# RWKV products stacked into wider matmuls with v centred beforehand, last units by row blocks, own banks for group 0, later root sum for mem

## What is computed

```python
def step(state, inp):                      # RWKV-7, per head, state 64x64
    r_t, w_t, k_t, v_t, a_t, b_t = inp
    sa = einsum('bhij,bhj->bhi', state, a_t)
    state = state * w_t + sa[..., None] * b_t + v_t[..., None] * k_t
    return state, einsum('bhij,bhj->bhi', state, r_t)
...
mean = y.mean(-1); var = ((y - mean) ** 2).mean(-1)
y = (y - mean) * rsqrt(var + B_GN_EPS) * ln_w + ln_b
return (y + sum(r * k * r_k) * v) * g
...
h = h + square(relu(xn @ mlp_w1)) @ mlp_w2
return rms_norm(h, norm_final)
```

## Time and profile before

| | |
|---|---|
| median of 3 runs | 2764.14 us (2763.07 to 2765.19) |
| profiled execution, its own time | 2762.59 us |
| span of that profile | 2760.9 us |
| TensorE busy | 2712.9 us (98%), granted clock 0.996 of 2.4 GHz |
| VectorE, ScalarE, GpSimd busy | 1236.4 (45%), 809.3 (29%), 132.9 us (5%) |

### The profile page before, as it was taken

How to read it: one execution, slowest core, us unless ns; L and a number is a source line. 1 busy time by engine, 2 the same in 40 slices (tenths; PEclk the granted TensorE clock), 3 DMA queues, 4 the chain that set the end, 5 groups by cost and what they waited for, 6 DMA issues and landing times.

```text
span 2760.9 us, 44373 instructions
## 1 busy us (share of the span) xinstructions
PE 2712.9 (98%) x18368; PEld 2158.3 (78%) x18368; DVE 1236.4 (45%) x1895; ACT 809.3 (29%) x1333; POOL 132.9 (5%) x237
## 2 busy tenths in 40 slices
PE   9999999999998999998999999999999999999997
PEld 7877777777777766786888888888888888888885
DVE  6266666666435545344433333333333333333333
ACT  5222222222124444243431221312213222122222
POOL 4000111001121100000000000000000000000000
PEclk9999999999999999999999999999999999999998
DMA  4311111111135422221233223322323323323322
GB/s 162 119 60 49 48 48 52 45 50 50 59 108 197 170 79 62 84 88 51 86 98 99 95 97 99 97 93 99 98 92 99 99 92 98 99 92 98 99 94 112
DMA packets 72396, 249.23 MB, mean 90 GB/s; under 512 B 8960, under 2 KB 9088, under 8 KB 71104
## 3 DMA queue, kind: packets, MB, share of 16 engines
q1 hardware_dynamic: 65232, 222.62, 25.3%
q0 software_dynamic: 7024, 24.56, 2.6%
HBM read 236.93 MB, written 10.22 MB: 90 GB/s over the span
## 4 chain that ended last, share of the span: by engine, by line
PE 94%; DVE 3%; issue 1%; DMA 1%; ACT 1%; DVEq 0%; SPq 0%; POOL 0%; ACTq 0%
PE ps L1141 28%; PE ps L1143 26%; PE ps L1142 26%; PE ps L1159 9%; PE ps L1375 1%; PE ps L1354 1%; PE ps L1363 1%; DMA h<-in_mem_turned 1%; PE ps L1153 1%; DVE w_lo L713 0%; PE ps L1214 0%; PE ps L1205 0%; PE ps L1194 0%; PE ps L1211 0%; PE ps L1220 0%
## 5 line engine op out<-in xcount | busy, mean ns | idle before, releaser
L713 DVE TENSOR_TENSOR w_lo<-w_raw,w_hi 128x1024 fp32r<-128x1024 f32 (+2 forms) x440 | 506.0, 1150 | 1143.4 <-ACT w_hi L432 1143.4
L432 ACT ACTIVATE w_hi<-w_raw 128x1024 fp32r<-128x1024 f32 (+2 forms) x440 | 439.0, 998 | 1539.3 <-PE ps L1143 1531.4
L1141 PE MATMUL ps<-act_hi,w_hi 128*128 128x512 f32 x1792 | 730.1, 407 | 1.1 <-DVE w_lo L713 1.1
L1143 PE MATMUL ps<-act_hi,w_lo 128*128 128x512 f32 x1792 | 700.1, 391 | 0.0
L1142 PE MATMUL ps<-act_lo,w_hi 128*128 128x512 f32 x1792 | 699.2, 390 | 0.0
L1141 PE MATMUL ps<-w_hi,mid_hi 128*128 128x512 f32 x1088 | 424.4, 390 | 1.4 <-DVE mid_lo L1087 1.4
L1143 PE MATMUL ps<-w_hi,mid_lo 128*128 128x512 f32 x1088 | 423.3, 389 | 0.0
L1142 PE MATMUL ps<-w_lo,mid_hi 128*128 128x512 f32 x1088 | 423.3, 389 | 0.0
L1141 PEld LDWEIGHTS ps<-act_hi,w_hi 128*128 128x128 f32 x1792 | 336.2, 188 | 93.7 <-issue 12.0
L1143 PEld LDWEIGHTS ps<-act_hi,w_lo 128*128 128x128 f32 x1792 | 336.5, 188 | 72.1
L1142 PEld LDWEIGHTS ps<-act_lo,w_hi 128*128 128x128 f32 x1792 | 336.8, 188 | 68.9 <-issue 6.0
(11 more groups left out here) (276 smaller groups left out, 2443.3 us busy)
## 6 DMA issues: line engine op xcount, KB each, us to landing
w_raw<-in_w_rest SPq DMA_DIRECT2D x320, 512.0 KB, 3.5
w_raw<-in_w_pairs SPq DMA_DIRECT2D x112, 384.0 KB, 3.0
x_t<-in_x_turned SPq DMA_DIRECT2D x8, 512.0 KB, 8.0
qk<-scr_qkv POOLq DMA_DIRECT2D x16, 256.0 KB, 3.6
h<-in_x POOLq DMA_DIRECT2D x4, 1024.0 KB, 11.1
out<-h SPq DMA_DIRECT2D x4, 1024.0 KB, 4.3
scr_qkv<-pad POOLq DMA_DIRECT2D x15, 256.0 KB, 3.8
w_raw<-in_w_lora SPq DMA_DIRECT2D x8, 288.0 KB, 7.1
```

The costliest lines, as they stand in the source:

```text
L432: return nc.scalar.activation(dst, src, ACT.Copy, scale=scale)
L713: V.tensor_tensor(dst, w_raw[:, slot, 0:dst.shape[-1]], high.bitcast(F32), ALU.subtract).then_inc(s["w_split"], 1)
L1141: mm(dst, a_hi, b_hi, start=start, stop=False)
L1143: return mm(dst, a_lo, b_hi, start=False, stop=stop)
```

## The change

It has six parts.

1. *Stacked products.* k and b lie side by side in `keys_b`. One product with 128 stationary columns (b and k) gives both Gram blocks of a head at once: with a (`gram_a`), with r (`gram_r`), and with the identity (`tok`, both turned to tokens). Each head has a bank of its own. The masks are applied to two banks at once. `keys_b` is written by halves (64 partitions each), so k x g_inv and b x g_inv become two VectorE instructions each.
2. *Chain.* u and v lie one above the other in `uv`. y takes one matmul per head over 128 rows, and so does the state. Bank 7 (`B_CHAIN`) holds all; y is copied out by VectorE after each chunk (L995 of the changed kernel). The v part of the next chunk's z moves from third 0 to the end of `chain_sy`, behind a wait of TensorE on its own y.
3. *Centred v.* v is turned to tokens with a centring matrix (`cen2`, identity less 1/64), which takes the place of the mean matmul, the copy of y and the subtraction for v; u comes out centred with it.
4. *Group 0* writes banks 4 to 6; its row sums move from position 18 to 21, its evacuation to unit 0 of group 1.
5. *mem*: sum over partitions, root and reciprocal move from positions 21 to 23 of group 14 to unit 2 of stage XK.
6. *End*: the gain is loaded early and multiplied into the first three quarters of h in the last chunk; the last two units are worked off by row blocks of 128 tokens, and each row tile is finished and stored by itself, ScalarE scaling 1536 columns, VectorE 512.

```diff
+            def stacked(b, rhs):
+                for c in range(NC):
+                    for hd, hf in enumerate(HALF):
+                        lhsT = keys_b[hf, c, :, :].rearrange("p i t -> p (i t)")
+                        last = mm(ps[:, b + hd, part(c)], lhsT, rhs(hf, c), start=True, stop=True)
+                return last
...
-                    mm(bank(3), mean2[:, :], yb[:, :], start=True, stop=True).then_inc(s["mean_mm"], 1)
...
-                    to_tokens(3, kk_dec).then_inc(s["ktok_mm"], 1)
-                if p == 10 and elem:
-                    pe.wait_ge(s["ab_ready"], q + 1)
-                    pe.wait_ge(s["ss_max"], q + 1)
-                    grams(4, kk_dec, aT[par]).then_inc(s["mak_mm"], 1)
-                if p == 11 and elem:
-                    pe.wait_ge(s["bon_ev"], q + 1)
-                    grams(5, kk_dec, rT[par]).then_inc(s["mrk_mm"], 1)
...
+                if p == 11 and elem:
                     pe.wait_ge(s["kt_ready"], q + 1)
+                    pe.wait_ge(s["ab_ready"], q + 1)
+                    pe.wait_ge(s["bt_ready"], q + 1)
+                    pe.wait_ge(s["ss_max"], q + 1)
+                    pe.wait_ge(s["bon_ev"], q + 1)
+                    stacked(B_W, lambda hf, c: aT[par][hf, part(c)]).then_inc(s["gram_a_mm"], 1)
...
-                grams(4, aT[par], aa).then_inc(s["mab_mm"], 1)
-                    pe.wait_ge(s["mrk_ev"], q + 1)
-                    grams(5, aa, aT[par]).then_inc(s["mabT_mm"], 1)
...
-                    to_tokens(3, aa).then_inc(s["btok_mm"], 1)
+                    pe.wait_ge(s["mab_ev"], q + 1)
+                    stacked(B_TOK, lambda hf, c: eye2[hf, :]).then_inc(s["tok_mm"], 1)
...
-                        grams(3, aa, rT[par]).then_inc(s["mrb_mm"], 1)
+                        stacked(B_TOK, lambda hf, c: rT[par][hf, part(c)]).then_inc(s["gram_r_mm"], 1)
...
             def chain_sy(c, u):
                 par = c % 2
                 pe.wait_ge(s["u_ev"], NC * c + u + 1)
-                if u < NC - 1:
-                    both(ps[:, 6, 2 * L:3 * L], b_tok[par][:, part(u)], u_s, True, False)
-                    both(ps[:, 6, 2 * L:3 * L], k_tok[par][:, part(u)], v_tok[par][:, part(u)], False, True).then_inc(s["s_mm"], 1)
...
+                dst = ps[:, B_CHAIN, 3 * L:4 * L]
+                for hd, hf in enumerate(HALF):
+                    last = mm(dst[hf], uv[par][:, hd, part(u)], m_r[par][:, hd, part(u)], start=True, stop=u == 0)
                 if u:
                     last = both(dst, st_s[:, u % 2, :], rT[par][:, part(u)], False, True)
-                if u == NC - 1:
+                if u < NC - 1:
                     last.then_inc(s["y_mm"], 1)
+                    for hd, hf in enumerate(HALF):
+                        mm(ps[hf, B_CHAIN, 2 * L:3 * L], tok[par][:, hd, part(u)], uv[par][:, hd, part(u)],
+                           start=True, stop=True)
+                    pe.wait_ge(s["y_mm"], (NC - 1) * c + u + 1)
+                    last = values_into_z(c, u + 1)
+                last.then_inc(s["sy_mm"], 1)
...
                 if p == 6 and elem:
                     dve.wait_ge(s["g_ready"], 2 * (q + 1))
-                    V.tensor_tensor(kk_dec[:, :], kp[:, :], g_inv[:, :], ALU.mult).then_inc(s["kt_ready"], 1)
+                    for hd, hf in enumerate(HALF):
+                        last = V.tensor_tensor(k_part(hd), chunks(kp)[hf], chunks(g_inv)[hf], ALU.mult)
+                    last.then_inc(s["kt_ready"], 1)
...
+            def last_units(n):
+                pe.wait_ge(s["w_split"], n + 2)
+                for t in range(TT):
+                    for u in range(2):
+                        wh = rest_slot(w_hi, u).rearrange("p (c n) -> p c n", c=2)
+                        wl = rest_slot(w_lo, u).rearrange("p (c n) -> p c n", c=2)
+                        for k in range(2):
+                            kt, tp = 4 + 2 * u + k, slice(t * P, (t + 1) * P)
+                            last = split_mm(bank(4 * ((S_MLP + 3) % 2) + t), mid_hi[:, kt, tp], mid_lo[:, kt, tp],
+                                            wh[:, k, :], wl[:, k, :], False, kt == FT - 1)
+                    last.then_inc(s["last_done"], 1)
...
+            def finish(t):
+                one, cols = slice(t, t + 1), slice(3 * 512, D)
+                dve.wait_ge(s["last_squares"], t + 1)
+                V.tensor_reduce(rms[:, one], ssq[:, one, :], axis=mybir.AxisListType.X, op=ALU.add)
+                dve.drain()
+                V.tensor_scalar(rms[:, one], rms[:, one], 1.0 / D, RMS_EPS, ALU.mult, ALU.add).then_inc(s["last_mean"], 1)
+                dve.wait_ge(s["last_sqrt"], t + 1)
+                V.reciprocal(rms[:, one], rms[:, 4 + t:5 + t]).then_inc(s["last_root"], 1)
+                dve.drain()
+                V.scalar_tensor_tensor(h[:, t, cols], h[:, t, cols], rms[:, one], gain_out[:, cols],
+                                       ALU.mult, ALU.mult).then_inc(s["out_ready"], 1)
```

More of the change, by code:

```diff
@@ L526, in position @@
                         act.wait_ge(s["y_fin"], f)
[L527 to L528 removed]
+                    act.wait_ge(s["y_ev"], NC * (f + 1))
+                    nc.scalar.activation(ysq[:, :], yy[f % 2][:, :], ACT.Square).then_inc(s["ysq_ready"], 1)
                 if p == 3 and elem:
                     act.wait_ge(s["vtok_mm"], q + 1)
[L531 removed]
+                    for hd in range(2):
+                        own, other = stack_of(hd)
+                        last = copy(uv[par][other, hd, :], ps[other, B_TOK, :])
+                    last.then_inc(s["vtok_ev"], 1)
                 if p == 4 and elem:
@@ L936, in _ @@
                     if g == 1 and u == 0:
+                        for m in range(3):
+                            evacuate(0, m)
                         dve.wait_ge(s["in_evac"], 3)
@@ L1165, in grams, with values @@
                 return last
-            def to_tokens(b, src):
+            def stacked(b, rhs):
                 for c in range(NC):
-                    last = both(ps[:, b, part(c)], src[:, part(c)], eye2, True, True)
+                    for hd, hf in enumerate(HALF):
+                        lhsT = keys_b[hf, c, :, :].rearrange("p i t -> p (i t)")
+                        last = mm(ps[:, b + hd, part(c)], lhsT, rhs(hf, c), start=True, stop=True)
+                return last
+            def values(b):
+                for c in range(NC):
+                    for hd in range(2):
+                        own, other = stack_of(hd)
+                        last = mm(ps[other, b, part(c)], vv[own, part(c)], cen2[own, :], start=True, stop=True)
                 return last
@@ L1250, in position @@
                         pe.wait_ge(s["x_ev"], (LV - 1) * q + lv)
-                    grams(4, m_abT, inv).then_inc(s["t_mm"], 1)
+                    for c in range(NC):
+                        for hd, hf in enumerate(HALF):
+                            last = mm(ps[hf, B_W, part(c)], m_a[par][hf, hd, part(c)], inv[hf, part(c)],
+                                      start=True, stop=True)
+                    last.then_inc(s["t_mm"], 1)
                 if p >= 15 and p % 2 == 1 and elem:
```

294 lines of the change are left out of this document (161 added, 133 removed).

## The result

| | before | after |
|---|---|---|
| median of 4 runs | 2764.66 us (2763.07 to 2765.67) | 2805.23 us (2803.42 to 2806.32) |
| span of the profile | 2760.9 us | 2804.6 us |
| TensorE busy, granted clock | 2712.9 us, 0.996 | 2743.6 us, 0.987 |
| VectorE, ScalarE busy | 1236.4, 809.3 us | 1259.2, 835.2 us |

The changed kernel takes 1.0147 times as long, 95% interval [1.0131, 1.0163], 40.6 us more. I had 2781 us and a range up to 2797: slower was right, the size was 24 us short.

A forecast was written before the change was run, and what follows sets the result against it. TensorE was taken to bound a full RWKV group, busy for all 75.74 us. The RWKV groups' +31 us and the other parts' -13.5 gave +17, some 2781 us for the median, with a range of 2748 to 2797.

The forecast's parts named there:

- (e): VectorE ahead of position 11: added half instructions delay bonus_v, so TensorE waits about 2.8 us in each group.
- if the clock falls to 1.2 GHz behind them as after rows 8: Rival: clock falls behind the position 11 waits, up to 1.7 us each; 2783 to 2796 us, 6%.
- A change of shape: TensorE switching tile shape: about 0.09 us plus an exposed first weight load of 0.05, so 0.15 us a change.
- the rival of 2791: Rival in chain_sy: column halves run one after the other, 0.23 us a part; 2791 us, 20%.
- (a): Mean matmul removed from a group: -0.84 us.
- (c): chain_sy, units 1 to 6: 0.63 becomes 0.96 us with column halves side by side; in sum +2.04 us.
- (d): Stacked products in a group: bound by weight loads, 1.82 us each against 0.93 for one; in sum +0.3 us.
- loads in the open: Rival in stacked products: 128-column load and matmul take turns, 2.6 us a product; 2799 us, 5%.
- shape costs nothing: Rival: shape changes are free and 128-column loads hide, so a stacked product takes 0.93 us; 2738 us, 12%.
- (b): z in units 1 to 7: third 0 loses a part of 0.12 us, -0.82 us in a group.
- (f): tok waits for m_ab's mask, as VectorE work queues behind gram_a: some 0.3 us in a group.
- Ends: Parts outside the RWKV groups: x sum -2.7, mem -4.4 and -1.6, end -7.5 and +2.7; in sum -13.5 us.

The follow-up runs named there:

- experiment 1: Changed kernel with eight unused main-like matmuls queued on TensorE ahead of gram_a's waits at position 11: 2784.71 us.
- experiment 2: Changed kernel with gram_a and its VectorE mask moved from position 11 to position 12: 2789.12 us.
- experiments 4: Kernel before with four unused 128x512 products added on VectorE ahead of bonus_v, forcing a wait at position 11: 2799.12 us.
- experiment 7: Three runs varying what TensorE does ahead of the wait: two on the kernel before (2788.65, 2788.78 us), one on the changed kernel (2818.85 us).
- experiment 11: Kernel before with parts 3 to 6 of the change: 2763.01 us; with TensorE's loop over the middle MLP chunks also written out: 2746.23 us.
- experiment 10: Changed kernel with r_dec, g_last and bonus_v after unit 3's state on VectorE, gram_a in banks 4 and 5 at position 12: 2764.27 us.
- e8_relieved: Changed kernel with GpSimd making the two k halves and gram_a in banks 4 and 5, free of bonus_v: 2793.68 us.
- e9_sy_order: e8_relieved with the two 128-row parts of chain_sy first and the two 64-row parts behind them: 2796.06 us.
- e10_wait_then_main: Changed kernel with the wait for bonus_v kept at position 11, but gram_a and its mask moved to position 12: 2813.25 us.
- e17_products_ahead: Changed kernel with unused 64x64 products at positions 9 and 10 and three more VectorE products ahead of bonus_v: 2818.85 us.
- e14_wait_moved: Kernel before with a_dec,k_dec moved behind the wait of position 11 and two products added on VectorE ahead of bonus_v: 2788.65 us.
- e16_both_behind: Kernel before with k turned to tokens and a_dec,k_dec both behind position 11's wait, one product added on VectorE: 2788.78 us.
- e15_wait_long: Kernel before with six unused 128x512 products added on VectorE ahead of bonus_v, for a longer wait at position 11: 2813.88 us.

## Why the prediction was wrong

**The step that failed** is the price of the wait (e). The sum put the clock behind it at nothing, and left it to a rival: "if the clock falls to 1.2 GHz behind them as after rows 8, up to 1.7 us each", with 6%. It falls behind every one of the eight, and a fall costs 3.0 us (2.94 in experiment 1, 3.04 in experiment 2). 2781 and 8 x 3.0 us make 2805. That this comes out to the microsecond is luck in part: the group came out 0.45 us cheaper than booked, the ends gained 2 us less, and the fall in group 3 cost more than 3. I had taken the price from the 4.3 us window behind the waits of the earlier trace rows, and the chance from the single wait of the earlier trace rows, behind which nothing happened. That row was true and told nothing of position 11: waits of 2.3 to 2.8 us sometimes bring the clock down and sometimes not, even from group to group of one kernel (experiments 4 and 7).

**Point by point.**
- *What bounds a group:* right. A wait of TensorE is time lost in full.
- *A change of shape, 0.15 us:* right. Parts of `chain_sy` are 0.26 us apart (four in 1.05 us, 469.79 to 470.84), with 0.12 of streaming. *Column halves side by side:* right; the rival of 2791 is out.
- *(a)* -0.84, measured -0.86 (75.74 to 74.88). *(c)* `chain_sy` from 0.63 to 1.05 with the change behind it, of which (c) has 0.96 and (d) 0.09: right. (The terms of (c), 0.17 + 3 x 0.27, make 0.98, not 0.96.)
- *(d)* stacked product 1.82 us and 0.1 for the change of shape: 1.93. Right; the rivals "loads in the open" (2.6 us) and "shape costs nothing" (0.93 us) are out.
- *(b), (c), (d) together* +1.5, and so they are: 82.09 less 2.73 idle, 2.94 for the clock and the 74.88 of experiment 11 is 1.54.
- *(e)* wait 2.8 us, measured 2.65; in group 3 nearly 5, measured 5.86. A half more costs 0.81 us (1.41 less 0.60), I had 0.78.
- *(f)* tok waits 0.3 us for the mask: wrong, it does not wait. A wait of 0.3 us stands elsewhere, for y_cent at unit 3, since a reciprocal lies ahead of the copy.
- *Sum of a group:* +3.8 predicted; 6.35 measured less 3.0 for the clock is +3.35.
- *Ends:* -13.5 predicted, -11.5 measured; 1.6 us is again the clock, behind the 2.46 us wait ahead of the last units. The sign "one wait, not two, around group 14, with the clock at 1.0" came half true: one wait, but the clock down behind it in this kernel (0.57 over 3.97 us) as before, and staying up in others (experiment 10). The wait for x_sum is gone and the first wait of XK is 2.67 us, both as foreseen, and from the last matmul to the end pass 11.7 us (2792.91 to 2804.6) where I had 11.9. (The terms as listed add up to 11.6, so the end should have been -7.8; and 12% with half of 12% is 18% for faster, not 17.)

Where the 59 us between the changed kernel and the best one lie: 24.6 waits (bonus_v, y_cent), 24 clock, and the remaining 10 or so TensorE's own work, of which (b), (c) and (d) give 1.5 us a group.

**What stays open:** how much of the difference between the changed kernel and its relatives (a fall behind every wait of 2.0 to 3.3 us) and the variants of the kernel before (behind some waits of 2.3 to 2.8 us) is the surroundings and how much the offset at which the waits begin (experiment 7). No run shifted the waits in time alone. Ruled out as the cause by themselves are the stacked product directly behind the wait, the short wait ahead of it, and the places of the side products.

## What to carry over

Where TensorE is the bound, moving work to VectorE ahead of a product that TensorE needs is paid twice: once as the wait and once as half-speed matmuls behind it, here 2.65 and 3.0 us. Price a new wait of some 2 us or more with the fall included, since here it came behind most of them, and look first for what VectorE can do after the product instead (experiment 10: 41 us by order and another pair of banks). Wider tiles save nothing when their weight loads are longer than what they stream, and each change of shape costs 0.15 us. Count the cases before comparing how often the clock falls: groups that repeat at nearly the same interval are one case many times over. Run the parts of a change alone: here four of six, with TensorE's loop written out, were worth 17 us together and hidden under the other parts' loss.

## What the hardware showed unexpectedly

- The fall of the clock behind the wait in groups 4 to 10 of each profile (the last four in the surroundings of the kernel before). A full fall cost about 3 us, a partial one 1.4 to 2. The last column is to be read with the offsets of experiment 7:

| kernel | wait, us, start to start | groups with a fall |
|---|---|---|
| e1_fill | 0.8 | none of 7 |
| e2_gram_later | 1.7 | 2 of 7, 2 more partly |
| e8_relieved | 2.0 | 4 of 7, 3 more partly |
| e9_sy_order | 2.0 | 5 of 7, 2 more partly |
| e10_wait_then_main | 2.6 | 5 of 7 (longer), 2 more partly |
| changed kernel | 2.65 | 7 of 7 |
| e17_products_ahead | 3.0 to 3.3 | 5 of 7, 2 more partly |
| e14_wait_moved (before) | 2.3 | 3 partly |
| e16_both_behind (before) | 2.5 to 2.8 | 2 partly |
| e7_wait (before) | 2.8 to 3.0 | 2 of 7, 1 more partly |
| e15_wait_long (before) | 4.4 | 5 of 7, 2 more partly |

- Which of seven like waits in one kernel bring the clock down goes with where on an even raster in time they begin (experiment 7).
- A loop turn of TensorE can stop it for 2.3 to 2.6 us, in one build of nearly the same program and not in another, and the trace then names an engine that had long been done.
- A copy of eight columns on VectorE took 1.24 instead of 0.16 us beside a GpSimd product.
